# Decay levels by in-place products, GLA heads in row pairs, conditioning steps between projections

## The chip, the cores and the metric

The program runs on one core of one Trainium2 chip. The metric is the device time of one execution in microseconds (us), lower is better. TensorE is called PE here, VectorE DVE, ScalarE ACT, GpSimd POOL; SP is the queue that issues the weight transfers.

## The reference, cut to what matters

One decoder layer (`DEPTH = 1`) for 256 prompt tokens and 8 sample tokens (one new token of each of 8 sequences, which have a stored state), width 1024, all in float32:

```python
mod = (silu(c) @ w_ada + b_ada)[:, None, :]           # w_ada 1024 x 6144: "conditioning"
sh1, sc1, g1, sh2, sc2, g2 = split(mod, 6)
h = rms_norm(x, norm1_g) * (1.0 + sc1) + sh1
hq, hf, hi, hg, gq, gk, gv, gg, gr = split(h @ w_in)  # 4 HGRN2 heads 128x128, 4 GLA heads 64x128
log_f = logaddexp(log(lb), log1p(-lb) + log_sigmoid(hf))      # k_h = (1-lb) * sigmoid(-hf)
log_a = log_sigmoid(gr @ w_gk2 + b_gk2) / 16.0                # gr has 16 columns
# per head and token: S_t = diag(a_t) S_{t-1} + k_t v_t^T ; o_t = S_t^T q_t, with a = exp(log_f) or exp(log_a)
x = x + g1 * (concat(o_h, o_g) @ w_o)                 # o after a head norm and a silu gate
h = rms_norm(x, norm2_g) * (1.0 + sc2) + sh2
x = x + g2 * moe_ffn(h)                               # 32 experts, top 4, clamped SwiGLU, D_FF = 1024
y = rms_norm(x, final_norm_g)
```

The new states of the prompt and of the 8 samples are outputs too.

## The kernel before

**Two parts.** A front (conditioning, projections, recurrence, output projection, router) is followed by 32 experts in a row, each of which is applied to a gathered block of 64 tokens. The weights go through one ring in SBUF of 16 slots of 1 MB. The front loads its 42 blocks of 1 MB through slots 0 to 7 in the order of the table `FRONT`: 24 blocks of w_ada (three rounds of 8), 14 of w_in (two for each group of 512 columns), 4 of w_o. SP issues them strictly in this order, and each waits until the block that was in its slot eight loads earlier has been used (L390). Slots 8 to 15 are scratch for the recurrence (`scr`: cumulated logs, level factors, attention, values, sample states). The experts take pairs of slots (L400): 6 loads of 2 MB for each expert. The first two go into slots 0 to 3 as these come free; the third waits for `heads_out` (the outputs of all heads have left scratch, L1564) and for the stored sample states, and the others follow.

**The order of the front.** The table `MIDDLE` gives the order of tasks on PE, ACT and DVE alike; each engine walks through it and does its share. Task names: `proj c i` is one of 28 projections of 128 columns, 8 matmuls (L904); `ada r` is a round of conditioning, 8 steps of 4 matmuls into four column groups (L861), and its transposition back (L870); `low` and `y` are the gate of rank 16 (L912, L916); `lev g l` is level l of the recurrence of group g (0: HGRN2, 1: GLA; L953, L945); `vt` turns the values to tokens (L928), `kdt` the decayed keys (L961); `state` makes the prompt's states (L968, L976); `so u` reads out the sample states of unit u (L1004, L1008), u = 0 to 3 an HGRN2 head, 4 and 5 a pair of GLA heads; `out` computes the heads' outputs (L991, L994). All 4 x 8 outputs of the groups go through three PSUM banks (`aux_bank`).

**The recurrence before.** With b the cumulated log decay in a chunk of 128 tokens, level 0 is the diagonal of the attention; level l = 1 to 7 covers pairs of tokens in neighbouring halves of a block of 2m, m = 1, 2, 4, ..., 64. For each level DVE subtracts b at the block's middle (L1382, L1384), ACT takes the exponential (L660), DVE multiplies q and k by it into copies (L1400, L1404, for GLA four masked copies, L1410), PE multiplies, and DVE takes the result over under a mask (L1424). GLA heads have 64 rows of keys: two lie in one tile of 128 rows, and a mask of halves makes a full copy for each.

**The sample states** are POOL's. For each unit u in turn it issues the load of the states and of the values, spread over all partitions from a buffer in DRAM (L511 to L517), waits for both, does three operations of 128x1024 (L523, L525, L526) and stores. There are two buffers, so unit u waits for the read-out of unit u-2:

```python
if u >= 2:
    pool.wait_ge(sem("osam_done"), u - 1)
```

Read literally, unit 2 starts after `so 0` on PE and unit 3 after `so 1`. In front of unit 0 and of unit 4 POOL writes the values of the group to DRAM and waits for that (L501).

## Time and profile before

| | |
|---|---|
| three runs | 2350.32, 2345.37, 1259.42 us; median 2345.37 us |
| the profiled execution | 1259.53 us, its span 1257.8 us |
| mean granted TensorE clock in it | 0.965 |
| PE busy | 1149.9 us (91%) |
| DVE busy | 440.0 us (35%) |
| ACT, POOL busy | 202.2 us, 66.0 us |
| moved by DMA | 460.80 MB, mean 366 GB/s |

All rows below are of the profiled execution. In the chain of waits each line is a stretch of the path that ended last: when it began, how long it took, which engine and line of the kernel it was spent on ("DMA" is a wait for a transfer). A timeline lists the instructions themselves.

### The profile page before, as it was taken

The numbers are of one execution on the slowest core, as the hardware profiler recorded it, in microseconds if no ns is written. First come the engines' busy times: TensorE is split into PE (matmuls) and PEld (weight loads), VectorE is DVE, ScalarE is ACT, GpSimd is POOL, SyncE is SP. The second block draws the span as 40 slices with busy tenths as digits, with TensorE's granted clock in tenths as the row PEclk, the third lists the DMA queues.
The fourth block names the chain that finished last, engine by engine and source line by source line (L and its number), as shares of the span: only waits on it lengthen the run. The fifth ranks groups of instructions, "written<-read, shape, count | busy, mean of one in ns | idle before, by whom it ended". The sixth has DMA issues, their size and how long they took to land.

```text
span 1257.8 us, 14110 instructions
## 1 busy us (share of the span) xinstructions
PE 1149.9 (91%) x5573; PEld 535.5 (43%) x5573; DVE 440.0 (35%) x805; ACT 202.2 (16%) x361; POOL 66.0 (5%) x75
## 2 busy tenths in 40 slices
PE   6997998988999999999999998999999999999995
PEld 4753887867433333333333333333333333333331
DVE  2123876533332233432222324232233322222224
ACT  2120321121211111211111111111111111111112
POOL 0003235200000000000000000000000000000001
PEclk9997997897999999999999998999999999999998
DMA  9869764463499999999999999999999999999994
GB/s 349 305 249 363 225 151 128 137 267 134 185 427 430 426 427 429 426 430 428 427 430 427 428 430 425 429 427 425 429 427 426 429 429 427 430 427 428 430 427 180
DMA packets 46628, 460.80 MB, mean 366 GB/s; under 512 B 6677, under 2 KB 7529, under 8 KB 18906
## 3 DMA queue, kind: packets, MB, share of 16 engines
q1 hardware_dynamic: 40600, 449.69, 85.5%
q0 software_dynamic: 2752, 9.47, 3.5%
q10 hardware_dynamic: 3234, 1.05, 0.4%
q8 instruction: 29, 0.48, 0.1%
q14 instruction: 13, 0.11, 0.0%
HBM read 455.55 MB, written 4.65 MB: 366 GB/s over the span
## 4 chain that ended last, share of the span: by engine, by line
PE 59%; DMA 33%; DVE 5%; ACT 2%; ACTq 1%; issue 1%; DVEq 0%; SPq 0%
DMA ring<-in_w_up 30%; PE bank L1133 21%; PE bank L1180 12%; PE bank L904 7%; PE bank L1169 3%; PE bank L1102 3%; DMA ring<-in_w_ada 2%; PE bank L1031 2%; PE bank L1149 2%; PE bank L945 1%; PE bank L1121 1%; PE bank L861 1%; PE bank L834 1%; DVE ring L1410 1%; DVE ring L1400 1%
## 5 line engine op out<-in xcount | busy, mean ns | idle before, releaser
L1133 PE MATMUL bank<-ring,arena 128*64 128x512 f32 x2048 | 459.1, 598 | 48.2 <-DMA ring<-in_w_up 46.9
L1133 PEld LDWEIGHTS bank<-ring,arena 128*64 128x64 f32 x2048 | 142.1, 137 | 358.1 <-issue 274.5
L1180 PE MATMUL bank<-ring,arena 128*64 128x512 f32 x1024 | 228.9, 600 | 1.7 <-DVE arena L1704 1.7
L1180 PEld LDWEIGHTS bank<-ring,arena 128*64 128x64 f32 x1024 | 71.2, 138 | 136.8 <-issue 123.8
L904 PE MATMUL bank<-arena,ring 128*128 128x264 f32 x448 | 109.5, 404 | 1.8 <-DVE arena L1343 1.8
L1684 DVE COPY arena<-bank 128x512 f32<-128x512 f32 x32 | 22.1, 691 | 237.7 <-PE bank L1133 237.7
L750 ACT ACTIVATE arena<-bank 128x512 f32<-128x512 f32 x32 | 19.1, 597 | 492.4 <-PE bank L1133 492.4
L904 PEld LDWEIGHTS bank<-arena,ring 128*128 128x128 f32 x448 | 88.2, 200 | 17.7 <-issue 2.4
L1736 DVE TENSOR_TENSOR arena<-bank,arena 128x512 f32<-128x512 f32 x32 | 22.1, 691 | 194.2 <-PE bank L1180 194.2
L1731 DVE TENSOR_TENSOR arena<-arena,bank 128x512 f32<-128x512 f32 x128 | 79.1, 680 | 1.5 <-PE bank L1169 1.5
L1693 DVE TENSOR_TENSOR arena<-bank,bupT 128x512 f32<-128x512 f32 x64 | 44.0, 687 | 71.0 <-PE bank L1149 71.0
L1169 PE MATMUL bank<-arena 64*128 64x512 f32 x256 | 63.6, 615 | 1.7 <-DVE arena L1747 1.7
L1102 PE MATMUL bank<-arena 128*64 128x512 f32 x256 | 60.5, 593 | 1.0 <-DVE arena L1633 1.0
L1639 DVE TENSOR_TENSOR arena<-arena 128x256 f32<-128x256 f32 x32 | 13.6, 425 | 103.8 <-PE bank L1158 103.7
L538 POOL TENSOR_TENSOR arena<-arena 128x512 f32<-128x512 f32 x1 | 1.3, 1262 | 925.2 <-DVE arena L1747 925.2
L764 ACT ACTIVATE arena<-bank 128x256 f32<-128x256 f32 x32 | 12.2, 382 | 212.8 <-PE bank L1158 212.8
L1149 PEld LDWEIGHTS bank<-ident,arena 128*128 128x128 f32 x256 | 33.2, 209 | 26.8 <-issue 25.2
L1149 PE MATMUL bank<-ident,arena 128*128 128x128 f32 x256 | 39.2, 296 | 0.8 <-ACT arena L750 0.8
L945 PE MATMUL bank<-ring 128*128 128x64 f32 x224 | 29.4, 288 | 10.2 <-DVE ring L1410 9.6
L861 PE MATMUL bank<-ring 128*32 128x512 f32 x192 | 26.3, 672 | 10.1 <-DMA ring<-in_w_ada 10.1
L945 PEld LDWEIGHTS bank<-ring 128*128 128x128 f32 x224 | 28.8, 205 | 13.2 <-DVE ring L1410 11.3
L1102 PEld LDWEIGHTS bank<-arena 128*64 128x64 f32 x256 | 18.4, 137 | 37.0 <-issue 35.9
(278 smaller groups left out, 842.3 us busy)
## 6 DMA issues: line engine op xcount, KB each, us to landing
ring<-in_w_up SPq DMA_DIRECT2D x128, 2048.0 KB, 33.7
ring<-in_w_down SPq DMA_DIRECT2D x64, 2048.0 KB, 31.3
ring<-in_w_ada SPq DMA_DIRECT2D x24, 1024.0 KB, 12.8
ring<-in_w_in SPq DMA_DIRECT2D x14, 1024.0 KB, 20.9
ring<-in_w_o SPq DMA_DIRECT2D x4, 1024.0 KB, 7.0
ring<-in_state_hgrn POOLq DMA_DIRECT2D x4, 512.0 KB, 7.6
arena<-sample_values POOLq DMA_DIRECT2D x4, 512.0 KB, 12.4
out_hgs<-ring POOLq DMA_DIRECT2D x4, 512.0 KB, 5.4
```

The lines of the kernel that those rows point to most:

```text
L861: last = mm(bank[32 * g:32 * g + 32, 1, :], siluT[:, k, :], ring[:, FRONT_SLOT[n], 512 * g:512 * g + 512], start=(k == 0), stop=(k == KT - 1))
L904: last = mm(bank[:, b, 0:T], ring[:, slot, 512 * (k % 4) + P * i:512 * (k % 4) + P * i + P], hT[:, k, :], start=(k == 0), stop=(k == KT - 1))
L945: last = mm(bank[:, b, P * h + 64 * c:P * h + 64 * c + 64], ks[:, l % 2, h, P * c:P * c + P], qs[:, l % 2, q0:q0 + 64], start=True, stop=True)
L1031: last = mm(bank[:, WO_BANK[m % 3], 0:T], ring[:, FRONT_SLOT[ld], D * (k % 2) + P * m:D * (k % 2) + P * m + P], oT[:, k, :], start=(k == 0 ...
L1102: last = mm(bank[64 * half:64 * half + 64, 6, :], pick[:, i, :], h2tok[:, i, 512 * half:512 * half + 512], start=(i == 0), stop=(i == 1))
L1133: last = mm(bank[64 * half:64 * half + 64, b, :], xe[:, par, k % 4, k // 4, :], pairs[:, slot, col:col + 512], start=(k == 0), stop=(k == ...
L1149: last = tr(bank[:, 2 + b, P * j:P * j + P], us[:, c0:c0 + 4 * P - 3:4], ident[:, :])
L1169: mm(bank[:, b, :], gpickT[64 * half:64 * half + 64, P * i:P * i + P], ysb[64 * half:64 * half + 64, :], start=True, stop=True).then_inc(s ...
L1180: last = mm(bank[64 * half:64 * half + 64, 5, :], actT[:, k, :], pairs[:, slot, D * kk + 512 * half:D * kk + 512 * half + 512], start=(k = ...
L1684: v.tensor_copy(us[:, 512:1024], bank[:, 1, :]).then_inc(sem("us_dve"), 1)
L1693: return TT(dst.rearrange("p (j h s) -> p j h s", j=4, h=2), bank[:, 2 + b, :].rearrange("p (j h s) -> p j h s", j=4, h=2), bias(b).to_bro ...
L1731: TT(y, y, bank[:, b, :], ALU.add).then_inc(sem("acc_used"), 1)
```

## The change

- `FRONT` and `MIDDLE`: the w_ada blocks of round 1 are loaded behind the first two column groups of w_in, those of round 2 behind two more; the conditioning steps stand two by two between projections, and `turn r` is the transposition back. The levels start in the third group of projections.
- The decays themselves take the place of their logs: ACT makes a = exp(log) once (`fT`), DVE makes the products over blocks of 2, 4, ..., 128 tokens (`spans_of`, seven dependent products), and before each level multiplies q in the later halves and k in the earlier halves in place (`level_up`). The exponentials of each level, the sums, the separate copies, `kmask`, `kd` and `qdec` go: q and k end as what `out` and `kdt` need.
- GLA heads are multiplied as row pairs: 64 rows of the tile each, into a bank each, with no masked copies. A GLA level takes two banks.
- `low` writes four groups of 32 columns at once and leaves their sum to `y`.
- The conditioning vectors are loaded as 72x128 and turned by one transposition; four steps of round 0 run ahead of the norm's sums. Small loads move from SP to ACT's queue, those for the gate and the router to later.
- In the code behind the 32 experts, for tokens beyond an expert's capacity, one wait and one count are added.

POOL's own list of instructions stays as it was: 6 units with the same waits on `osam_done`. Only the place of `so 0` to `so 5` among PE's tasks moves.

```diff
 FRONT = ([("ada", 0, k) for k in range(8)]
-         + [("in", c, s) for c in (1, 0, 2) for s in range(2)]
-         + [("ada", 1, k) for k in range(8)] + [("ada", 2, k) for k in range(8)]
-         + [("in", c, s) for c in (4, 5, 3, 6) for s in range(2)]
+         + [("in", c, s) for c in (1, 0) for s in range(2)]
+         + [("ada", 1, k) for k in range(8)]
+         + [("in", c, s) for c in (2, 4) for s in range(2)]
+         + [("ada", 2, k) for k in range(8)]
+         + [("in", c, s) for c in (5, 3, 6) for s in range(2)]
          + [("out", 0, s) for s in range(4)])
...
-MIDDLE = ([("proj", c, i) for c in (HF, HQ, HI) for i in range(4)]
-          + [("ada", 1), ("vt", 0), ("ada", 2)]
-          + [("low",), ("lev", 0, 0), ("proj", GQK, 0), ("lev", 0, 1), ("proj", GQK, 1), ("lev", 0, 2),
-             ("proj", GQK, 2), ("lev", 0, 3), ("proj", GQK, 3), ("lev", 0, 4), ("y", 0), ("y", 1), ("proj", GV, 0),
-             ("lev", 0, 5), ("proj", GV, 1), ("lev", 0, 6), ("so", 0), ("proj", GV, 2), ("lev", 0, 7)]
-          + [("proj", GV, 3), ("so", 1), ("vt", 1)]
-          + [("proj", HG, 0), ("lev", 1, 0), ("proj", HG, 1), ("lev", 1, 1), ("kdt",), ("proj", HG, 2), ("lev", 1, 2),
-             ("so", 2), ("proj", HG, 3), ("lev", 1, 3), ("proj", GG, 0), ("lev", 1, 4), ("so", 3), ("proj", GG, 1),
-             ("lev", 1, 5), ("proj", GG, 2), ("lev", 1, 6), ("proj", GG, 3), ("lev", 1, 7),
-             ("state",), ("so", 4), ("so", 5), ("out",)])
+MIDDLE = ([("proj", HF, i) for i in range(4)]
+          + [t for i in range(4) for t in (("proj", HQ, i), ("ada", 1, 2 * i), ("ada", 1, 2 * i + 1))]
+          + [("turn", 1), ("proj", HI, 0), ("proj", HI, 1), ("lev", 0, 0), ("proj", HI, 2), ("lev", 0, 1),
+             ("proj", HI, 3), ("lev", 0, 2), ("low",), ("vt", 0), ("proj", GQK, 0), ("ada", 2, 0), ("ada", 2, 1),
+             ("lev", 0, 3), ("proj", GQK, 1), ("ada", 2, 2), ("ada", 2, 3), ("y", 0), ("y", 1),
+             ("lev", 0, 4), ("proj", GQK, 2), ("ada", 2, 4), ("ada", 2, 5), ("lev", 0, 5),
+             ("proj", GQK, 3), ("ada", 2, 6), ("ada", 2, 7), ("lev", 0, 6), ("turn", 2),
+             ("proj", GV, 0), ("lev", 0, 7), ("proj", GV, 1), ("lev", 1, 0), ("proj", GV, 2), ("lev", 1, 1),
+             ("proj", GV, 3), ("lev", 1, 2), ("vt", 1), ("proj", HG, 0), ("lev", 1, 3), ("proj", HG, 1), ("lev", 1, 4),
+             ("proj", HG, 2), ("so", 0), ("lev", 1, 5), ("proj", HG, 3), ("lev", 1, 6), ("proj", GG, 0), ("lev", 1, 7),
+             ("proj", GG, 1), ("kdt",), ("so", 1), ("proj", GG, 2), ("state",), ("so", 2), ("proj", GG, 3),
+             ("so", 3), ("so", 4), ("so", 5), ("out",)])
...
     if task[0] == "lev":
-        return 2 if task[2] == 0 else 1
+        return 2 if task[2] == 0 or task[1] == 1 else 1
...
-            act.wait_ge(sem("craw_zero"), 1)
-            act.dma_start(craw[0:1, :], a["c_prompt"]).then_inc(sem("c_in"), 16)
-            act.dma_start(craw[1:1 + TS, :], a["c_sample"]).then_inc(sem("c_in"), 16)
+            act.dma_start(craw[0:8, :], a["c_prompt"].rearrange("b (k p) -> (b k) p", p=P)).then_inc(sem("c_in"), 16)
+            act.dma_start(craw[8:72, :], a["c_sample"].rearrange("b (k p) -> (b k) p", p=P)).then_inc(sem("c_in"), 16)
...
-            act.dma_start(wgr, a["w_in"][0].rearrange("(k p) n -> p k n", p=P)[:, :, 3584:3600]).then_inc(sem("gr_in"), 16)
-            act.dma_start(wgk2, a["w_gk2"][0]).then_inc(sem("gr_in"), 16)
-            act.dma_start(wrt[:, :, :], a["router_w"][0].rearrange("(k p) n -> p k n", p=P)).then_inc(sem("router_in"), 16)
-            act.dma_start(brt[:, :], a["router_b"].to_broadcast([P, NE])).then_inc(sem("router_in"), 16)
...
-                if task == ("proj", HI, 3):
                     act.wait_ge(sem("logk_ready"), 1)
+                    od.did(A(fT[:, 0:4, :], fT[:, 0:4, :], ACT.Exp), sem("f_ready"))
                     od.did(A(kT[:, 0:4, :], kT[:, 0:4, :], ACT.Exp), sem("k_ready"))
-                    od.did(A(decay_s[:, 0:4, :], logf[:, 0:4, TP:T], ACT.Exp), sem("decay_s_ready"))
-                if task[0] == "ada":
-                if task[0] == "lev" and task[2] < 7:
-                    levels += 1
-                    act.wait_ge(sem("level_sub"), levels)
-                    v = level_factors(task[1], task[2] + 1)[2]
-                    od.did(A(v, v, ACT.Exp), sem("level_exp"))
...
-                if task == ("proj", GV, 3):
+                if task == ("turn", 2):
-                    od.did(A(decay_s[:, 4:6, :], logf[:, 4:6, TP:T], ACT.Exp), sem("decay_s_ready"))
-                    act.wait_ge(sem("kd_sub"), 1)
-                    od.did(A(kd[:, :, :], kd[:, :, :], ACT.Exp), sem("kd_exp"))
-                    od.did(A(decay_c[:, :], bT[:, :, TP - 1], ACT.Exp), sem("kd_exp"))
-                    od.did(A(qdec[:, 0:NQ, :], bT[:, :, P:TP], ACT.Exp), sem("kd_exp"))
+                    od.did(A(fT[:, 4:6, :], fT[:, 4:6, :], ACT.Exp, scale=1.0 / 16.0), sem("f_ready"))
+                if task == ("proj", GV, 2):
+                    act.dma_start(wrt[:, :, :], a["router_w"][0].rearrange("(k p) n -> p k n", p=P)).then_inc(sem("router_in"), 16)
+                    act.dma_start(brt[:, :], a["router_b"].to_broadcast([P, NE])).then_inc(sem("router_in"), 16)
...
-                        pe.wait_ge(sem("gr_in"), 32)
+                        pe.wait_ge(sem("gr_in"), 80)
-                            last = mm(bank[0:16, b, 0:T], wgr[:, k, :], hT[:, k, :], start=(k == 0), stop=(k == KT - 1))
+                            j = k % 4
+                            last = mm(bank[32 * j:32 * j + 32, b, 0:T], wgr[:, k, :], hT[:, k, :], start=(k < 4), stop=(k >= 4))
                         last.then_inc(sem("proj_psum"), 1)
...
+                    elif l == 0:
+                        pe.wait_ge(sem("proj_sb"), PROJ_AT[("proj", GQK, 3)] + 1)
+                        pe.wait_ge(sem(f"level_ready{g}"), 2 * l - 1)
+                    def later(x):
+                        return halves(x, l)[:, 0, :, 1, :] if l else x[:, 0, :]
+                    n = 64 if l else P
+                    if g == 1:
+                        banks = [aux_bank(), aux_bank()]
+                        for q in range(2):
+                            for c in range(NC):
+                                tt = slice(P * c, P * c + P)
+                                for i in range(2):
+                                    own = slice(64 * i, 64 * i + 64)
+                                    c0 = n * (2 * q + c)
+                                    last = mm(bank[:, banks[i], c0:c0 + n], kT[own, 4 + q, tt], later(qT[own, 4 + q:5 + q, tt]),
+                                              start=True, stop=True)
+                                    if (q, c) == (1, 1):
+                                        last.then_inc(sem("aux_psum"), 1)
...
+                    if u == 4:
+                        pe.wait_ge(sem("qsam_ready"), 4)
...
+            def spans_of(g):
+                n0, n1 = (0, 4) if g == 0 else (4, 6)
+                for l in range(1, 8):
+                    od.settle()
+                    x = spans[l - 1][:, n0:n1].rearrange("p n (q f) -> p n q f", f=2)
+                    od.did(TT(spans[l][:, n0:n1], x[:, :, :, 0], x[:, :, :, 1], ALU.mult))
+            def level_up(g, l):
+                n0, n1 = (0, 4) if g == 0 else (4, 6)
+                q, k = qT[:, n0:n1, 0:TP], kT[:, n0:n1, 0:TP]
+                ready = sem(f"level_ready{g}")
                 od.settle()
                 if l == 0:
+                    od.did(TT(q, q, fT[:, n0:n1, 0:TP], ALU.mult), ready)
                 else:
                     m = LEVELS[l - 1]
+                    shape = [P, n1 - n0, TP // (2 * m), m]
+                    x = spans[l - 1][:, n0:n1].rearrange("p n (q f) -> p n q f", f=2)
+                    late, early = halves(q, l)[:, :, :, 1, :], halves(k, l)[:, :, :, 0, :]
+                    od.did(TT(late, late, x[:, :, :, 0].unsqueeze(3).to_broadcast(shape), ALU.mult), ready)
+                    od.did(TT(early, early, x[:, :, :, 1].unsqueeze(3).to_broadcast(shape), ALU.mult), ready)
+            def level_take(g, l):
+                banks = [aux_in() for _ in range(aux_units(("lev", g, l)))]
+                level_up(g, l)
+                for n, b in enumerate(banks):
+                    own = slice(4 + 2 * n, 6 + 2 * n) if g else slice(0, 4)
+                    if l == 0:
+                        dst = att[:, own] if g else att[:, own, n, :]
+                        src = bank[:, b, :].rearrange("p (h t) -> p h t", h=4)
+                        if g:
+                            dst = dst.rearrange("p h c t -> p (h c) t")
+                        od.did(TT(dst, src, ident[:, :].unsqueeze(1).to_broadcast([P, 4, P]), ALU.mult), sem("aux_used"))
+                    else:
+                        m, x = LEVELS[l - 1], 4 if g else 8
+                        od.did(v.copy_predicated(
+                            att[:, own].rearrange("p h c (q f i) -> p (h c) q f i", f=2, i=m)[:, :, :, 1, :],
+                            level_mask[:, l - 1, :].rearrange("p (q f i) -> p q f i", f=2, i=m)[:, :, 1, :].unsqueeze(1)
+                            .to_broadcast([P, x, P // (2 * m), m]),
+                            bank[:, b, 0:64 * x].rearrange("p (x q i) -> p x q i", x=x, i=m)), sem("aux_used"))
```

**PE, from the read-out of the second sample unit to the outputs of the heads.** L1004 and L1008 in the kernel before are the read-outs (`so`), L904 a projection, L945 a level, L961 `kdt`, L968 and L976 `state`, L991 `out`. Before, from `so 1` on:

```order
L1004 MATMUL bank<-arena,ring 128x1 x8
L928 MATMUL bank<-ident,arena 128x128 x8
L928 MATMUL bank<-ident,arena 8x128 x4
L904 MATMUL bank<-arena,ring 128x264 x8
L953 MATMUL bank<-arena 128x128 x8
L904 MATMUL bank<-arena,ring 128x264 x8
L945 MATMUL bank<-ring 128x64 x8
L961 MATMUL bank<-ident,arena 128x128 x12
L904 MATMUL bank<-arena,ring 128x264 x8
L945 MATMUL bank<-ring 128x64 x8
L1004 MATMUL bank<-arena,ring 128x1 x8
L904 MATMUL bank<-arena,ring 128x264 x8
```

and its end, from `so 3` on:

```order
L1004 MATMUL bank<-arena,ring 128x1 x8
L904 MATMUL bank<-arena,ring 128x264 x8
L945 MATMUL bank<-ring 128x64 x8
L904 MATMUL bank<-arena,ring 128x264 x8
L945 MATMUL bank<-ring 128x64 x8
L904 MATMUL bank<-arena,ring 128x264 x8
L945 MATMUL bank<-ring 128x64 x8
L968 MATMUL bank<-ring 128x128 x8
L976 MATMUL bank<-ring 64x128 x8
L1008 MATMUL bank<-qsam,ring 128x2 x16
L991 MATMUL bank<-ring 128x128 x5
```

Of the change, from the last level on, where L918 is a projection, L968 a GLA level, L993 `kdt`, L1045 and L1049 read-outs, L1000 and L1008 `state`, L1020 `out`:

```order
L968 MATMUL bank<-arena 128x64 x8
L918 MATMUL bank<-arena,ring 128x264 x8
L993 MATMUL bank<-ident,arena 128x128 x12
L1045 MATMUL bank<-arena,ring 128x1 x8
L918 MATMUL bank<-arena,ring 128x264 x8
L1000 MATMUL bank<-ring 128x128 x8
L1008 MATMUL bank<-ring 64x128 x8
L1045 MATMUL bank<-arena,ring 128x1 x8
L918 MATMUL bank<-arena,ring 128x264 x8
L1045 MATMUL bank<-arena,ring 128x1 x8
L1049 MATMUL bank<-qsam,ring 128x2 x16
L1020 MATMUL bank<-ring 128x128 x5
```

Before, eight projections and eight levels lie behind `so 1`; now `so 1` has two projections behind it, and all levels lie ahead.

**PE, from the conditioning round 0 to the first values.** Before (L861 conditioning, L870 its transposition, L904 projections, L928 `vt`):

```order
L861 MATMUL bank<-ring 32x512 x32
L870 MATMUL bank<-ident,ring 128x128 x4
L904 MATMUL bank<-arena,ring 128x264 x96
L861 MATMUL bank<-ring 32x512 x32
L870 MATMUL bank<-ident,ring 128x128 x4
L928 MATMUL bank<-ident,arena 128x128 x8
L928 MATMUL bank<-ident,arena 8x128 x4
L861 MATMUL bank<-ring 32x512 x32
L870 MATMUL bank<-ident,ring 128x128 x4
```

Of the change (L853 conditioning, L884 its transposition, L918 projections, L977 level 0):

```order
L884 MATMUL bank<-ident,ring 128x128 x4
L918 MATMUL bank<-arena,ring 128x264 x40
L853 MATMUL bank<-ring 32x512 x8
L918 MATMUL bank<-arena,ring 128x264 x8
L853 MATMUL bank<-ring 32x512 x8
L918 MATMUL bank<-arena,ring 128x264 x8
L853 MATMUL bank<-ring 32x512 x8
L918 MATMUL bank<-arena,ring 128x264 x8
L853 MATMUL bank<-ring 32x512 x8
L884 MATMUL bank<-ident,ring 128x128 x4
L918 MATMUL bank<-arena,ring 128x264 x16
L977 MATMUL bank<-arena 128x128 x8
```

Rounds 1 and 2 stood together behind twelve projections; now round 1 lies between the projections of the second group, and its last two steps with the transposition stand right behind them.

**SP, the front's loads.** `waits` names what a load waits for. Of the change:

```order
L407 DMA ring<-in_w_in 128x4x512 [waits weights_used] x4
L407 DMA ring<-in_w_ada 128x2048 [waits weights_used] x3
L407 DMA ring<-in_w_ada 128x2048 [waits ada_psum]
L407 DMA ring<-in_w_ada 128x2048 [waits weights_used]
L407 DMA ring<-in_w_ada 128x2048 [waits proj_psum]
L407 DMA ring<-in_w_ada 128x2048 [waits weights_used]
L407 DMA ring<-in_w_ada 128x2048 [waits proj_psum]
L407 DMA ring<-in_w_in 128x4x512 [waits weights_used] x4
```

The last two w_ada loads of a round take the slots of the projection group that runs right ahead of the steps that use them, and the next w_in blocks stand behind them in SP's queue.

## Rows read from the trace of the kernel before

**Rows 1.** the page: the whole span, and GB/s in 40 equal slices
```profile
span 1257.8 us, 14110 instructions
...
GB/s 349 305 249 363 225 151 128 137 267 134 185 427 430 426 427 429 426 430 428 427 430 427 428 430 425 429 427 425 429 427 426 429 429 427 430 427 428 430 427 180
```

**Rows 2.** windows: start:end, us, busy (count) by engine, clock, DMA share, GB/s
```profile
400.00:500.00 100.00, 100.00 (x475) 36.35 (x472) 31.10 (x55) 12.63 (x23) 0.00 (x0) 1.00 1.01 428
```

**Rows 3.** DMA issues: what, queue, count, KB each, median us to landing
```profile
ring<-in_w_up SPq DMA_DIRECT2D x128, 2048.0 KB, 33.7
ring<-in_w_down SPq DMA_DIRECT2D x64, 2048.0 KB, 31.3
```

**Rows 4.** chain of waits: start us, us, what; last read-outs to first expert
```profile
241.80 4.89 PE bank L1008 x32
246.69 2.34 PE bank L991 x10
...
255.01 0.23 DVE arena L1564
...
325.70 15.65 PE bank L1133 x64
```

**Rows 5.** chain of waits, opening of the kernel up to the third projection group
```profile
14.79 1.22 DVE ring L1301
...
25.48 7.05 PE bank L861 x64
...
35.69 44.66 PE bank L904 x192
80.36 7.11 DMA ring<-in_w_ada
...
110.24 1.98 PE bank L861 x8
```

**Rows 6.** chain of waits: projection, level, sample read-out; an expert's combine
```profile
121.49 3.56 PE bank L904 x16
125.06 1.73 PE bank L945 x16
...
166.64 1.68 PE bank L1004 x16
```

**Rows 7.** timeline of DVE and ACT behind the second projection group
```profile
72.75 1.26 DVE L1461 TENSOR_TENSOR arena<-arena 128x1056 f32<-128x1056 f32 x1
...
80.72 1.07 ACT L650 ACTIVATE arena<-arena 128x1056 f32<-128x1056 f32 x1
```

**Rows 8.** timeline of POOL: start us, us, instruction, idle before it, releaser
```profile
175.35 0.88 POOL L511 DMA_DIRECT2D ring<-in_state_hgrn  x1
...
186.92 1.89 POOL L523 TENSOR_TENSOR arena<-arena 128x1024 f32<-128x1024 f32 x1 [9.81 <-DMA arena<-sample_values]
...
194.64 0.54 POOL L501 DMA_DIRECT2D sample_values<-ring  x1
...
210.62 1.90 POOL L523 TENSOR_TENSOR arena<-arena 128x1024 f32<-128x1024 f32 x1 [6.29 <-DMA arena<-sample_values]
...
218.61 0.70 POOL L511 DMA_DIRECT2D ring<-in_state_gla  x1
...
227.95 1.89 POOL L523 TENSOR_TENSOR arena<-arena 128x1024 f32<-128x1024 f32 x1 [6.60 <-DMA arena<-sample_values]
...
234.67 1.43 POOL L528 DMA_DIRECT2D out_gls<-ring  x2 [0.29 <-POOL ring L526]
```

**Rows 9.** timeline of DVE: one operation, POOL idle and POOL at work
```profile
179.82 0.42 DVE L1400 TENSOR_TENSOR ring<-arena,ring 128x256 f32<-128x256 f32 x1
...
187.03 2.06 DVE L1400 TENSOR_TENSOR ring<-arena,ring 128x256 f32<-128x256 f32 x1
```

**Rows 10.** a projection that began at the lower clock, and that stretch
```profile
200.92 6.46 PE bank L904 x16
...
190.00:204.00 14.00, 10.07 (x39) 9.35 (x40) 8.56 (x15) 1.84 (x5) 7.23 (x8) 0.60 0.21 59
```

356 lines of the change are left out of this document (150 added, 206 removed).

## The prediction

> **What bounds the kernel now.** I read the windows first. While the experts run, DMA is busy throughout and moves 428 GB/s [rows 1, 2]. Their weights are (128 + 64) transfers of 2048 KB, 402.7 MB [rows 3], and 402.7 MB at 428 GB/s are 941 us. PE runs beside it with less work than that: it is full only as long as the loads fetched ahead last. The 192 loads are six for each of 32 experts, so the code for overflowing tokens isn't entered. The change leaves this part alone, so its end follows one point: when the first expert starts and ring pairs come free. That is at 325.7 us; the heads are finished (L1564) at 255.2 us [rows 4], and the same instructions fill the 70.5 us between. So a microsecond by which the heads are finished earlier or later should be a microsecond of the whole. Everything in dispute lies before 255.2 us.
>
> The chain through the front shows why it takes that long. PE starts the projections at 35.7 us, does the first twelve in 44.7 us, and then waits for w_ada: rounds 1 and 2 end at 112.2 us instead of 80.4 us plus 14 us of work [rows 5]. From there PE is nearly full, with waits for DVE while POOL works.
>
> **The change part by part.** Times below are counted from the start of the span.
>
> *Opening.* ACT made three operations of 32x1024 behind its queue of DMA issues, DVE one, and PE's wait for it ended at 16.0 us [rows 5]. These become 72x128, about an eighth of the elements, and half of round 0 (7.05 us in all) runs ahead of the norm's sums. But w_ada's own 8.4 MB behind 1 MB of x, at the 349 GB/s of the first slice [rows 1], land only near 27 us, and about 1 us of conditioning and 3.2 us of copy, transposition and scaling follow as before. I take the first projection at 32.5 us (gain 3.2); bounds 31.2 and 35.7.
>
> *Groups HF and HQ.* Eight projections at 44.66 / 12 = 3.72 us are 29.8, six conditioning steps at 7.05 / 8 = 0.88 are 5.3: T1 = 67.6.
>
> *First refill.* Steps 6 and 7 of round 1 need slots that the projections of HQ right ahead of them free. The trace has this very pattern: two w_ada blocks behind twelve projections, the last one in after 7.1 us [rows 5]. The next blocks in SP's order are 1.05 MB each, 2.45 us at 428 GB/s; both HI blocks are in at T1 + 12.0. ACT agrees: it now makes both exponentials (1.07 us each) ahead of the copy for the transposition. DVE's last operation on the logs ended 8.6 us behind HQ (35.7 + 8 x 3.72 = 65.4 against 74.0) [rows 7]; plus 2.2 for the exponentials and 1.3 for copy and transposition that is T1 + 12.1. PE does the rest of HI 0 by T1 + 16.0 = 83.6.
>
> *Work to the end of GQK.* Seven projections 26.0, six conditioning steps 5.3, six levels at 1.73 10.4 [rows 6]. `vt` has twelve small matmuls and is put at a level's 1.7; `low` in four column groups and `y` are ten more, concurrent or short, at 1.0 each. Sum 45.4, T2 = 129.0. DVE's share for an HGRN2 level is two multiplications and the take-over, 512 elements each, about 0.7 between the rows of 256 and of 1056 elements [rows 7, 9], against 5.5 us of PE between two levels, and hides; if it didn't, PE would wait for it. The ACT exponentials of levels, DVE's sums, scans and masked copies that go are off PE's path, except where POOL is at work. New ahead of level 0 are seven dependent products of some 1,000 elements in all, about 2 us by the row of 1056, beside HI's projections.
>
> *Second refill.* Steps 6 and 7 of round 2 behind GQK: the same pattern, 7.1 us, with the last GV block in at T2 + 12.0; GV 0 ends, with the level ahead of it, at T2 + 14.5 = 143.5.
>
> *Work to `so 1`.* Nine projections 33.5, one HGRN2 level 1.7, eight GLA levels, `vt` and `kdt` 1.7 each, two read-outs at 1.68 3.4 [rows 6]. A GLA level keeps its eight matmuls, now with 64 rows. The nearest row for such pairs is the experts' combine, eight with 64 rows and 512 columns in 1.92 us [rows 6]; bounds for a level are half of 1.73 and 2.0; I take 1.4, so 11.2. Sum 53.2: 196.7. To this I add 5 us of waits and lower clock, bounds 0 and 14 (three times the clash and twice the clock that follow). A DVE operation took 0.42 us with POOL idle and 2.06 us with POOL at work [rows 9], and three POOL units now fall into the levels. A projection that began at the lower level took 6.46 us against 3.56; the granted clock in 190 to 204 us was 0.60, behind two waits of PE [rows 6, 10]; its two levels are 2.4 and 1.2 GHz, and each refill is such a wait. `so 1` ends at about 202.
>
> *The sample states.* Here the change gives the gain back. Unit 3 needs `so 1`, 4 follows 3, 5 follows 4, all on POOL, whose own work isn't changed. The rows give the price: from the issue of unit 3 (175.35) to the end of unit 5 (0.3 before 234.67) 59.0 us. In it are 9.81, 6.29 and 6.60 us of waits for transfers, three times 6.4 of arithmetic, and the detour of group 1's values through DRAM, 194.64 to over 200 [rows 8]. Before, `so 1` ended at 168.3 us [rows 6] and eight projections and eight levels covered the 59 us; POOL ended at 234.4, and PE came to the last two units at 241.8 [rows 4]. Now PE has two projections, `state` and four read-outs to put over them, some 20 us. So PE waits: 202 + 0.5 + 59 = 261.5. Unit 2 doesn't add: `so 0` ends 19 us ahead of `so 1`, and unit 2 takes the 18 of unit 3 (175.35 to 193.4) and its store. Then come `so 5` (half of 4.89), `out` and the last copies (246.7 to 255.2 before, 8.5 us [rows 4]; I take 11 behind such a long wait): 275. Against 255.2 this is +19.8. For a clock that stays low a little into the norm I add 1.5. The profiled execution's own time is 1259.53, 1.7 above its span: 1259.5 + 21.3 = **1281 us**.
>
> One rule would make the chain shorter. The waits of POOL for its transfers were 9.81, 6.29 and 6.60 us, for 1 MB and twice 0.5 MB [rows 8]. The Trainium skill ("DMA: Bandwidth & Descriptors", section on the anatomy of one DMA) gives about 2.0 us plus bytes / 436e3 for one DMA; by it these waits would be 4.4, 3.2 and 3.2 us, the chain 47 us and the time about 1269. The trace disagrees with it for these spread-out values of 512 bytes, and I go by the rows.
>
> The rest is small: router and gate weights move to later on ACT's queue and are covered by the projections that stand ahead of their users; if that were gone, each would cost about the 7.1 us of a load that PE waits for. `so 4`'s new wait on the masked queries is over long before.
>
> **The rivals.**
> - *The state chain doesn't decide* (0.12). Then PE's own work does: 202 + 3.7 + 3.5 (`state`, sixteen matmuls, as two levels) + 1.7 + 3.7 + 1.7 + 4.9 + 8.5 = 229.7, 25.5 us earlier than before: 1234. For it: DVE lies idle there, nothing slows POOL. Against: 59 us are three times what PE has left; the chain would have to fall to under 30.
> - *The balance is nearly even* (0.12), 1250 to 1265: GLA levels at half price (4 us), no waits (5 us), transfers of the states at 6 us (3 us), refills shorter by some.
> - *`so 1` comes late* (0.18), 1294 to 1310: since all of POOL's chain hangs on it, each wait of PE ahead of it is paid in full, and so it decides the sign beyond 2% from about 206 us on. The clash of DVE and POOL, 6.4 us of slowed DVE in each of three units, would hold PE up by up to some 4 us each time, while GLA levels stand in line for their banks, and the clock would follow.
> - *That the change isn't what it says*: order shows the read-outs where I put them; I give this nothing.
>
> The forecast itself, 1266 to 1294, has 0.58.
>
> **How the numbers follow.** What a measurement of this kernel can tell from no change is about 2%, 25 us, so the limits are 1234 and 1285. Faster: a half of the first rival, 0.06. Slower: nearly all of the third, 0.17, and the upper 0.4 of the forecast, 0.24, in all 0.41. The rest, 0.53, lies within. The likeliest case's own range is 1266 to 1294, that of all cases 1245 to 1300. The sum stands against 1259.53 us, the profiled execution, with which one of the three runs (1259.42) agrees; the median shown, 2345.37, is that of the other two, 1.86 times longer. Such a ratio is near that of the two clock levels, and I can't tell from one profile which of them a median of the changed kernel will hit; I give the longer 0.35. There the front's PE work doubles and POOL's chain doesn't, so my gain and loss would lie between 2345 - 45 and 2345 + 45, about twice the limits above. A range that leaves out no more than 2 in 10 has to reach that far: 1245 to 2390.
>
> **What would show it.** In the changed trace: the first projection near 32.5 us; waits for w_ada of some 5 to 7 us behind HQ and behind GQK; read-out L1045 waiting for POOL at the fourth, fifth and sixth unit, with PE nearly idle from about 217 to 261 us; heads finished near 275 and the first expert's L1174 near 346. I am wrong if PE doesn't wait for POOL there, if `so 1` ends before 190 or after 210, or if the experts don't shift one for one with the heads.

## The result and the profile after

The changed kernel takes 1283.63 us (median of 4 runs, 1282.61 to 1285.38). Its ratio to the kernel before is **1.0177, 95% interval 1.0118 to 1.0237**: slower; whether by more or less than 2% is not settled. Beside it the kernel before ran in two groups again (1252.69 and 1259.42, 2345.37 and 2350.32); the ratio leaves the long group out, no run of the changed kernel fell into it, and against the two short runs alone it would be 1.022. The profiled execution took 1283.37 us.

The page of the kernel after, the rows that answer to [rows 1]:

```profile
span 1281.5 us, 14019 instructions
...
PEclk9989899569799999999999999899999999999999
...
GB/s 347 292 321 107 313 174 153 149 124 186 106 378 429 428 426 428 427 429 429 428 429 429 429 428 429 428 426 428 428 427 429 426 430 429 428 429 428 429 429 181
```

The full rate of 428 GB/s begins one slice later than before; behind it the rates are the same within 2 GB/s. A slice is 32 us, and the change lies in that one and the slices ahead of it. PE's waits (in total, times, longest):

```profile
PE bank L1174 <- DMA ring<-in_w_up: 47.9, 41, 1.3
PE bank L1049 <- POOL ring L543: 31.3, 2, 17.4
PE bank L853 <- DMA ring<-in_w_ada: 18.4, 5, 10.2
...
PE bank L1045 <- POOL ring L543: 4.6, 1, 4.6
```

35.9 us of waits for POOL in the sample read-outs. They lie here (timeline of PE, the last projections to the output products):

```profile
206.23 1.50 PE L993 MATMUL bank<-ident,arena 128*128 128x128 f32 x12 [2.94 <-issue]
207.56 1.84 PE L1045 MATMUL bank<-arena,ring 128*128 128x1 f32 x16
209.27 3.81 PE L918 MATMUL bank<-arena,ring 128*128 128x264 f32 x16
...
226.00 3.58 PE L1045 MATMUL bank<-arena,ring 128*128 128x1 f32 x16 [4.57 <-POOL ring L543]
246.94 3.55 PE L1049 MATMUL bank<-qsam,ring 128*128 128x2 f32 x16 [17.36 <-POOL ring L543]
264.43 3.57 PE L1049 MATMUL bank<-qsam,ring 128*128 128x2 f32 x16 [13.94 <-POOL ring L543]
```

The first row is `kdt`, the second `so 1`, the last three are `so 3`, `so 4` and `so 5`. POOL's timeline shows what they wait for, and answers to [rows 8]:

```profile
187.58 0.88 POOL L528 DMA_DIRECT2D ring<-in_state_hgrn  x1 [38.96 <-PE bank L1045]
...
209.72 0.88 POOL L528 DMA_DIRECT2D ring<-in_state_hgrn  x1 [2.64 <-PE bank L1045]
...
219.72 1.89 POOL L540 TENSOR_TENSOR arena<-arena 128x1024 f32<-128x1024 f32 x1 [8.24 <-DMA arena<-sample_values]
...
231.84 0.73 POOL L528 DMA_DIRECT2D ring<-in_state_gla  x1 [4.12 <-DMA sample_values<-ring]
...
240.63 1.89 POOL L540 TENSOR_TENSOR arena<-arena 128x1024 f32<-128x1024 f32 x1 [5.94 <-DMA arena<-sample_values]
...
258.21 1.89 POOL L540 TENSOR_TENSOR arena<-arena 128x1024 f32<-128x1024 f32 x1 [6.99 <-DMA arena<-sample_values]
...
264.67 1.43 POOL L545 DMA_DIRECT2D out_gls<-ring  x2 [0.29 <-POOL ring L543]
```

POOL stood idle for 38.96 us until `so 0` freed a buffer. Then units 3, 4 and 5 followed each other from 209.72 to 264.4 us, 54.7 us, and PE had 12 us of projections, `state` and `so 2` (209.27 to 221.4) to put over them. In the windows (columns as in [rows 2]) PE does 0.58 us of work in 17, and its clock falls to the lower level:

```profile
229.00:246.00 17.00, 0.58 (x3) 0.49 (x3) 0.00 (x0) 0.00 (x0) 8.06 (x7) 0.50 0.37 89
```

The chain of waits, which answers to [rows 4], runs from POOL through `so 5` into the experts:

```profile
262.04 2.35 POOL ring L543
264.43 3.57 PE bank L1049 x16
268.00 2.34 PE bank L1020 x10
...
350.88 13.95 PE bank L1174 x64
```

### The profile page after: what moved, and what is told of

It is laid out like the page before. It is cut to its first block, busy times and chain, and to the rows that moved or that the text cites. A ratio compares the mean times of both kernels' runs of the same rounds, so it can differ in the third digit from the quotient of the medians.

```text
span 1281.5 us, 14019 instructions
## 1 busy us (share of the span) xinstructions
PE 1134.8 (89%) x5566; PEld 518.7 (40%) x5566; DVE 393.8 (31%) x756; ACT 189.0 (15%) x344; POOL 65.6 (5%) x75
## 4 chain that ended last, share of the span: by engine, by line
PE 46%; DMA 30%; DVE 1%; ACT 1%; POOL 0%; issue 0%; SPq 0%; DVEq 0%; ACTq 0%
DMA ring<-in_w_up 30%; PE bank L1174 20%; PE bank L1221 12%; PE bank L1143 3%; PE bank L1210 3%; PE bank L1072 2%; PE bank L1190 2%; PE bank L1162 1%; PE bank L1199 1%; DMA arena<-sample_values 1%; PE bank L1090 0%; PE bank L1116 0%; PE bank L1020 0%; PE bank L1049 0%; PE bank L1056 0%
## 5 line engine op out<-in xcount | busy, mean ns | idle before, releaser
L918 PE MATMUL bank<-arena,ring 128*128 128x264 f32 x448 | 108.5, 399 | 1.8 <-DVE arena L1382 1.8
L918 PEld LDWEIGHTS bank<-arena,ring 128*128 128x128 f32 x448 | 85.7, 196 | 19.4 <-issue 4.6
L555 POOL TENSOR_TENSOR arena<-arena 128x512 f32<-128x512 f32 x1 | 1.3, 1267 | 925.3 <-DVE arena L1732 925.3
L853 PE MATMUL bank<-ring 128*32 128x512 f32 x192 | 28.3, 712 | 18.8 <-DMA ring<-in_w_ada 18.4
L1049 PE MATMUL bank<-qsam,ring 128*128 128x2 f32 x32 | 7.1, 352 | 31.3 <-POOL ring L543 31.3
L1210 PEld LDWEIGHTS bank<-arena 64*128 64x128 f32 x256 | 26.8, 185 | 16.6 <-issue 10.5
```

Source lines behind the costliest of these rows:

```text
L853: last = mm(bank[32 * g:32 * g + 32, 1, :], siluT[:, k, :], ring[:, FRONT_SLOT[n], 512 * g:512 * g + 512], start=(k == 0), stop=(k == KT - 1))
L918: last = mm(bank[:, b, 0:T], ring[:, slot, 512 * (k % 4) + P * i:512 * (k % 4) + P * i + P], hT[:, k, :], start=(k == 0), stop=(k == KT - 1))
L1210: mm(bank[:, b, :], gpickT[64 * half:64 * half + 64, P * i:P * i + P], ysb[64 * half:64 * half + 64, :], start=True, stop=True).then_inc(s ...
```

## The experiments

The yardstick is DVE's copy of the sample columns ("heads"), the last thing before the norm; before it began at 255.0 us, after at 278.3 us (278.28, L1549). "Heads" and the spans are those of one profiled execution of each kernel; the medians are over all its runs. The kernel before, timed beside each group of experiments, had medians of 1260.09, 1261.38 and 1260.53 us.

### so_early: only the read-outs move back

```diff
-             ("proj", GV, 0), ("lev", 0, 7), ("proj", GV, 1), ("lev", 1, 0), ("proj", GV, 2), ("lev", 1, 1),
+             ("proj", GV, 0), ("lev", 0, 7), ("so", 0), ("proj", GV, 1), ("lev", 1, 0), ("so", 1), ("proj", GV, 2), ("lev", 1, 1),
...
-             ("proj", GG, 1), ("kdt",), ("so", 1), ("proj", GG, 2), ("state",), ("so", 2), ("proj", GG, 3),
-             ("so", 3), ("so", 4), ("so", 5), ("out",)])
+             ("so", 3), ("proj", GG, 1), ("kdt",), ("proj", GG, 2), ("state",), ("proj", GG, 3),
+             ("so", 4), ("so", 5), ("out",)])
```

`so 2` stands behind `lev 1 4`, and the places between projections where the change had `so 0` to `so 2` are empty.

> The changed kernel with its read-outs moved: so 0 and so 1 right behind GV 0 and GV 1, so 2 behind the fifth GLA level, so 3 behind the last level. Theory (POOL's chain of sample states, 55 us from so 1 to the end of unit 5, sets the end): it starts near 155 instead of 209.7 us, unit 5 is ready near 231 us, heads at about 245, time about 1250 us. Rival (the levels, the refills or the clock set the end, and the read-outs wait only beside it): less than 10 us gained, 1274 us or more.

1256.85 us (10 runs), ratio 0.9967 (0.9931 to 1.0002). Heads at 251.7 us, 26.6 us earlier than in the change, and the span is shorter by 27.0 us. That is the theory's way, though 245 and 1250 had been expected. One wait for POOL is left:

```profile
PE bank L1049 <- POOL ring L543: 6.8, 1, 6.8
```

So the whole loss is the read-outs' place. But the rest of the change, which I had counted as a gain, brought only 3.3 us over the kernel before, and the ratio's interval reaches 1.

### before_so_late: the kernel before with late read-outs

```diff
-             ("lev", 0, 5), ("proj", GV, 1), ("lev", 0, 6), ("so", 0), ("proj", GV, 2), ("lev", 0, 7)]
-          + [("proj", GV, 3), ("so", 1), ("vt", 1)]
...
+             ("lev", 0, 5), ("proj", GV, 1), ("lev", 0, 6), ("proj", GV, 2), ("lev", 0, 7)]
+          + [("proj", GV, 3), ("vt", 1)]
+          + [("proj", HG, 0), ("lev", 1, 0), ("proj", HG, 1), ("lev", 1, 1), ("kdt",), ("proj", HG, 2), ("so", 0), ("lev", 1, 2),
...
+             ("so", 1), ("lev", 1, 5), ("proj", GG, 2), ("lev", 1, 6), ("so", 2), ("proj", GG, 3), ("lev", 1, 7),
+             ("state",), ("so", 3), ("so", 4), ("so", 5), ("out",)])
```

> The kernel before with nothing changed but the place of so 0 to so 3: as late among the projections as the change has them (so 0 behind HG 2, so 1 behind GG 1, so 2 behind GG 2, so 3 behind the last level). Theory: so 1 ends near 218 us, POOL's chain of 55 to 59 us ends near 275, heads near 289 instead of 255, time about 1292 us (1283 to 1300). Rival (the cost comes with the new arithmetic or the interleaved conditioning): no change, 1259 us.

1287.22 us (4 runs), ratio 1.0177 (1.0099 to 1.0255). Nothing of the new arithmetic is in it, and the same wait stands in the same place:

```profile
PE bank L1008 <- POOL ring L526: 31.8, 2, 17.8
```

Heads at 289.9 us, 34.9 us late, span 34.7 us longer. The profiled execution (1294.36 us) was the slowest of the four; the medians differ by 27 us.

### five_buffers: the late read-outs stay, the buffers don't run out

```diff
-        Ssam = scr[:, 13312:15360].rearrange("p (u b v) -> p u b v", u=2, b=TS)
+        NSB = 5
+        Ssam = [scr[:, c:c + 1024].rearrange("p (b v) -> p b v", b=TS) for c in (13312, 14336, 15360, 3584, 4864)]
...
-                if u >= 2:
-                    pool.wait_ge(sem("osam_done"), u - 1)
+                if u >= NSB:
+                    pool.wait_ge(sem("osam_done"), u - NSB + 1)
```

> The changed kernel in its own order, with five buffers for the sample states instead of two, so that only unit 5 waits for a read-out (so 0). Theory: POOL runs its units through and is done near 224 us, PE meets all read-outs ready; its waits of 36 us behind so 1 go, heads near 241, time about 1245 us (1240 to 1250). Rival (POOL's transfers and arithmetic are the bound themselves, not the wait for the read-outs): 1270 us or more.

1258.74 us (10 runs, one of them 1484.87), ratio 0.9963 (0.9927 to 1.0000). The mechanism is confirmed: with buffers to spare the same late order costs nothing against before. The expected 1245 is missed, though. The profiled execution, at 1267.47 us, is 9 us above the median, so its rows may show more waiting than most runs had. PE's wait for POOL became shorter but not gone:

```profile
PE bank L1050 <- POOL ring L544: 20.1, 1, 20.1
```

POOL itself is the next bound. It cannot start before unit 0's values are turned (109.7 us), and from the third on a unit takes 22 to 25 us beside the weight loads, with waits for transfers of 12.6 to 16.4 us.

### new_arith_old_order: the arithmetic alone

```diff
-MIDDLE = ([("proj", HF, i) for i in range(4)]
-          + [t for i in range(4) for t in (("proj", HQ, i), ("ada", 1, 2 * i), ("ada", 1, 2 * i + 1))]
+MIDDLE = ([("proj", c, i) for c in (HF, HQ, HI) for i in range(4)]
+          + [("ada", 1, k) for k in range(8)] + [("turn", 1), ("vt", 0)] + [("ada", 2, k) for k in range(8)] + [("turn", 2)]
...
```

Levels, read-outs and the order of the loads are those of the kernel before; only `kdt` stands behind the last level and `y` behind GQK 1.

> The in-place products, row pairs and column groups of the change, in the order of the kernel before: rounds 1 and 2 of the conditioning together behind twelve projections, read-outs where they were; kdt behind the last level, the gate's y behind GQK 1. Theory: the arithmetic by itself gains the DVE waits (about 10 us), 0.7 us for each of 8 GLA levels and some 4 us of the low-rank gate, while the pause of 32 us stays: 1243 us (1238 to 1250), with no long wait for POOL. Rival (the new arithmetic costs DVE or PE time): 1262 us or more.

1252.80 us (10 runs), ratio 0.9946 (0.9909 to 0.9983). Heads at 244.7 us, 10.3 us earlier than before, and no wait for POOL. The times gain less (7 us between the medians, 6.9 between the spans), and 1243 had been expected. POOL starts at 89.85 us:

```profile
89.85 0.72 POOL L514 DMA_DIRECT2D sample_values<-ring  x1 [85.95 <-DVE ring L1488]
```

The products of block decays and the row pairs are a gain, then. In so_early the heads are 7 us later than here. The two kernels differ in the order of conditioning and projections, but also in the places of levels and read-outs, so these 7 us are not shown to be the first alone; between the spans they are 3.6, because the first expert's 64 matmuls (L1170) took 16.85 us here, at 0.82 granted, and 13.95 in so_early, at 1.00.

### short_units: shorter work in the chain

```diff
+                if u < 3:
+                    od.did(g.tensor_tensor(vbc[:, :, :], vbc[:, :, :],
+                                           kT[:, u, TP:T].unsqueeze(2).to_broadcast([P, TS, P]), ALU.mult))
+                    od.link(g.tensor_tensor(S, S, fT[:, u, TP:T].unsqueeze(2).to_broadcast([P, TS, P]), ALU.mult))
```

> The change, with GpSimd's two multiplications left out in units 3 to 5 (the sample states of those units keep only their load and the addition, so part of the decode states isn't computed). Nothing else moves. In the change's trace the chain from the issue of unit 3's load (209.72) to the end of unit 5's work (264.4) is what the fourth, fifth and sixth read-outs wait for (4.6, 17.4 and 13.9 us). Theory 1 (the state chain, one unit after another behind the late second read-out, ends the stage): three units lose some 3.8 us each, the chain 11.3 us, the heads and the end come 11 us earlier: about 1272 us. Theory 2 (the projections and conditioning matmuls set the stage, and the waits for GpSimd would only be replaced by others): no more than 3 us, 1280 to 1283.

1278.44 us (2 runs), ratio 1.0126 (1.0075 to 1.0177); heads at 271.8 us, 6.5 us earlier than in the change, not 11. Its POOL rows say why:

```profile
212.45 0.88 POOL L528 DMA_DIRECT2D ring<-in_state_hgrn  x1 [2.64 <-PE bank L1046]
...
234.26 0.74 POOL L528 DMA_DIRECT2D ring<-in_state_gla  x1 [7.75 <-DMA sample_values<-ring]
...
258.99 1.40 POOL L546 DMA_DIRECT2D out_gls<-ring  x2 [0.29 <-POOL ring L544]
```

Unit 3 was issued 2.7 us later than in the change, and the values' detour through DRAM waited 7.75 us instead of 4.12. From issue to end the chain takes 46.3 us instead of 54.7, 8.4 shorter; less the 2.7 that is 5.7, and the heads moved by 6.5. Theory 2 (at most 3 us) is out, and theory 1's 11 us are missed. The chain sets the end; what a cut of it gives back also depends on the transfers. Why the detour took longer was not tested.

### no_interleave: conditioning steps in one piece

```diff
-MIDDLE = ([("proj", HF, i) for i in range(4)]
-          + [t for i in range(4) for t in (("proj", HQ, i), ("ada", 1, 2 * i), ("ada", 1, 2 * i + 1))]
+MIDDLE = ([("proj", c, i) for c in (HF, HQ) for i in range(4)]
+          + [("ada", 1, k) for k in range(8)]
...
-             ("lev", 0, 4), ("proj", GQK, 2), ("ada", 2, 4), ("ada", 2, 5), ("lev", 0, 5),
-             ("proj", GQK, 3), ("ada", 2, 6), ("ada", 2, 7), ("lev", 0, 6), ("turn", 2),
...
+             ("lev", 0, 4), ("proj", GQK, 2), ("lev", 0, 5), ("proj", GQK, 3)]
+          + [("ada", 2, k) for k in range(8)]
+          + [("lev", 0, 6), ("turn", 2),
```

> The change with the conditioning steps 0 to 7 of groups 1 and 2 put together again behind the four projections of their stage (HQ and GQK) instead of two between each pair; the read-outs of the sample states, the levels and their arithmetic stay as in the change. Theory 1 (each refill of the conditioning weights waits for the slots that the steps free, and is covered less or more by what runs beside it, and GpSimd's start hangs on the value turn of unit 0): the stage loses waits for GpSimd's start of some 10 us, the second read-out and the chain behind it come about 10 us earlier, 1273 us. Theory 2 (the place of the conditioning steps is worth nothing, only the place of the read-outs is): 1281 to 1285, as the change.

1272.74 us (6 runs), ratio 1.0092 (1.0059 to 1.0125). Heads at 266.8 us, 11.5 us earlier, as theory 1 said. POOL started 7.0 us earlier, and unit 3's load was issued at 197.58 instead of 209.72 us, right behind unit 2 and without a wait for `so 1`. With the steps between the projections PE has used them up when the refill's last blocks are still on their way; in one piece, most of the steps run while it loads. In the changed kernel the last blocks of group 1 and of group 2 (timeline of PE):

```profile
73.71 1.07 PE L853 MATMUL bank<-ring 128*32 128x512 f32 x8 [3.38 <-DMA ring<-in_w_ada]
77.86 1.94 PE L853 MATMUL bank<-ring 128*32 128x512 f32 x8 [3.09 <-DMA ring<-in_w_ada]
...
143.67 1.94 PE L853 MATMUL bank<-ring 128*32 128x512 f32 x8 [10.22 <-DMA ring<-in_w_ada]
```

and in no_interleave, where seven of the eight steps of group 2 (56 matmuls) run in one piece ahead of the last; 4.49 us of waiting come behind it, for the values' weights:

```profile
120.20 6.22 PE L854 MATMUL bank<-ring 128*32 128x512 f32 x56
128.39 1.27 PE L854 MATMUL bank<-ring 128*32 128x512 f32 x8 [1.98 <-DMA ring<-in_w_ada]
...
138.61 5.86 PE L919 MATMUL bank<-arena,ring 128*128 128x264 f32 x16 [4.49 <-DMA ring<-in_w_in]
```

### combined and combined_late_loads

`combined` is no_interleave with five buffers, the read-outs of so_early, and `so 4`, `so 5` behind `out`. The second also holds back SP:

```diff
                 elif expert_slot(i) < 4:
+                    if i == 0:
+                        sp.wait_ge(sem("Ssam_ready"), NQ)
                     for half in range(2):
```

> The conditioning steps put together as in no_interleave, the read-outs 0 to 3 each as soon as its unit is ready and the last two behind the output products, and five buffers for the sample states instead of two. Theory 1 (the two causes, the late start of GpSimd and the read-outs' hold on the buffers, add up, and the last two units lie behind work that does not need them): the heads start at about 237, the time is 1241 us. Theory 2 (GpSimd's own chain of load, work and store beside the experts' first weights stays the bound, as in five_buffers): 1250 to 1258.

1247.51 us (4 runs), ratio 0.9881 (0.9843 to 0.9919); heads at 241.7 us, 5 later than expected, with 11.1 us of waiting for POOL. The time lies between the two theories.

> As combined, but SyncE issues the experts' first two weight loads only when the sample states of the last unit are ready. Theory 1 (the transfers of the states are slow because they share the DMA engines with these weights): units fall from some 25 us to some 17, and the time is 1235 to 1240 us, a few us below combined. Theory 2 (the first experts would then wait for their weights): the first expert's products start later by as much as the weights come late, 1245 to 1255 us, at or above combined.

1246.29 us (4 runs), ratio 0.9864 (0.9824 to 0.9904), which can't be told from combined. The transfer of unit 4 did what theory 1 says. First combined, then combined_late_loads (POOL's timeline):

```profile
210.01 1.89 POOL L542 TENSOR_TENSOR arena<-arena 128x1024 f32<-128x1024 f32 x1 [15.24 <-DMA arena<-sample_values]
```

```profile
201.96 1.89 POOL L544 TENSOR_TENSOR arena<-arena 128x1024 f32<-128x1024 f32 x1 [6.42 <-DMA arena<-sample_values]
```

POOL was done 12.5 us earlier, but PE came to the last two read-outs at 233.59 instead of 225.03 us. It was 2.4 us behind when the projection after `so 3` began, which took 5.40 us where combined had 3.81; a wait for DVE ahead of the last output products was 3.47 instead of 2.01 us, and these products ran at a granted 0.56 (226 to 234 us, PE busy 7.45 of 8). Theory 2's wait for the experts' weights did not appear: PE's waits for w_up are 46.9 us in all, against 47.3 in combined. What POOL's chain gave back, PE's own pace took; why the pace fell was not tested.

### early_values, and with late loads

Against combined, cut:

```diff
-         + [("in", c, s) for c in (1, 0) for s in range(2)]
+         + [("in", c, s) for c in (1, 0, 2) for s in range(2)]
...
-MIDDLE = ([("proj", c, i) for c in (HF, HQ) for i in range(4)]
-          + [("ada", 1, k) for k in range(8)]
+MIDDLE = ([("proj", c, i) for c in (HF, HQ, HI) for i in range(4)]
+          + [("ada", 1, k) for k in range(8)]
+          + [("turn", 1), ("vt", 0), ("lev", 0, 0), ("low",), ("proj", GQK, 0), ("lev", 0, 1), ("proj", GQK, 1), ("y", 0), ("y", 1),
...
```

The weights of HI are loaded ahead of round 1 with it, and every level stands one or two projections later than in combined.

> As combined (new arithmetic, five buffers, read-outs early, the last two behind the output products), and the four HI projections come before the conditioning steps of group 1 again, as in the kernel before, so that the value turn of unit 0 needs only the steps ahead of it. Theory 1 (combined is still bound by GpSimd's chain, whose start, 103, hangs on that turn): GpSimd starts at about 90, its last unit is ready before the output products end (225), the heads follow the last two read-outs at about 231, the time is 1236 us. Theory 2 (what is left is TensorE's own work at its clock, as combined_late_loads suggests, where GpSimd was 13 us earlier and the time the same): 1245 to 1248 us.

1239.14 us (4 runs), ratio 0.9844 (0.9793 to 0.9894); heads at 234.7 us, with 7.0 us of waiting for POOL left. POOL started at 91.9 us as expected, but its last unit was ready at 231.0, not before 225.

> As early_values, with SyncE's first two weight loads for the experts held until the last unit's sample states are ready. Theory 1 (with GpSimd's chain off the path by 10 us the transfers' sharing of the DMA engines no longer matters): as early_values within 3 us. Theory 2 (the chain is still the bound): 5 us below it.

**1235.09 us** (4 runs), ratio 0.9809 (0.9755 to 0.9863), heads at 228.0 us, no wait for POOL left. This is the fastest version. The intervals of the two ratios overlap, but the runs themselves don't (1231.96 to 1238.10 against 1238.16 to 1240.63 us), so the 4 us between the medians are likely real, and near theory 2's 5; the heads moved by 6.7 us. Its read-outs behind the output products took 3.80 us for both units, where one unit alone took 3.57 us at the lower clock in the change:

```profile
223.73 0.49 PE L1035 MATMUL bank<-arena 64*128 64x128 f32 x2
224.15 3.80 PE L1051 MATMUL bank<-qsam,ring 128*128 128x2 f32 x32
229.38 2.92 PE L1058 MATMUL bank<-arena,ones 128*128 128x512 f32 x3 [1.43 <-ACT arena L701]
```

All profiled executions together, in us. "POOL ends" is the end of the last unit's arithmetic:

| kernel | POOL starts | POOL ends | heads | span | span less heads |
|---|---|---|---|---|---|
| before | 92.6 | 234.4 | 255.0 | 1257.8 | 1002.8 |
| the change | 108.1 | 264.4 | 278.3 | 1281.5 | 1003.2 |
| so_early | 109.1 | 237.7 | 251.7 | 1254.5 | 1002.8 |
| before_so_late | 95.5 | 277.7 | 289.9 | 1292.5 | 1002.6 |
| five_buffers | 109.7 | 249.0 | 262.7 | 1265.4 | 1002.7 |
| new_arith_old_order | 89.9 | 230.3 | 244.7 | 1250.9 | 1006.2 |
| short_units | 107.7 | 258.7 | 271.8 | 1275.8 | 1004.0 |
| no_interleave | 101.1 | 252.6 | 266.8 | 1272.1 | 1005.3 |
| combined | 103.0 | 238.0 | 241.7 | 1245.2 | 1003.5 |
| combined_late_loads | 103.3 | 225.5 | 240.6 | 1246.8 | 1006.2 |
| early_values | 91.9 | 231.0 | 234.7 | 1237.7 | 1003.0 |
| early_values_late_loads | 90.1 | 219.5 | 228.0 | 1233.9 | 1005.9 |

The last column lies at 1002.6 to 1004.0 or at 1005.3 to 1006.2 us. In the four kernels with the higher values the first expert's 64 matmuls took 16.57 to 16.85 us, in the others 13.95 or 15.65.

## Why the prediction was right or wrong

**The mechanism held; that the time fits within 3 us is in part luck.** Forecast 1281, measured 1283.63. PE was 10 us later than forecast when GV 0 ended, and shorter levels (2.5) and a shorter chain on POOL (4.4) took most of that back. Point by point, against the trace after:

- *Bound and one-for-one shift*: right. The last column of the table stays within 1002.6 and 1006.2 us while the heads move over 62 us.
- *Opening*: wrong by all of it. I took the first projection at 32.5 us; it began at 35.46, as before. The shorter ACT work did get out of the way (PE's wait for it is gone), but conditioning went on waiting for its own weights: the last block's step began at 31.18 us behind 1.17 us of waiting for w_ada. Behind it came 1.07 us of conditioning and 3.2 us of copy, transposition and scaling, as I had them. The landing is what failed: I divided w_ada's and x's 9.4 MB by 349 GB/s, but by 31.2 us 10.8 MB had moved (345 GB/s in that window). SP had issued w_in from 17.01 us on, so its blocks were among them; no run held them back.
- *First refill*: the waits were 3.38 and 3.09 us (7.1 predicted). HI 0 started at 81.77 and ended at 87.4 (ACT's copy of it began at 87.47), against 83.6. The opening explains 3 us of that; the rest is the clock, 0.50 granted in 81.7 to 85.5 us, which the sum had left out here.
- *Second refill*: 7.1 us taken, 10.2 measured, and GV 0 ended at 153.6 instead of 143.5. GQK had ended 4.4 us late (133.4 against 129.0), so this stage lost 5.7. The trace of before showed this pattern with POOL idle. Here POOL issued the state load of unit 1 and its broadcast at 128.09 and 128.96 us, just ahead of the refill; the DMA engines were busy at 0.96 in 130 to 143 us and moved only 220 GB/s, against 362 in the first refill (windows; the columns are those of [rows 2]). That was the term with the largest error, and no row of mine counted POOL's transfers against PE's. That they are the cause is argued from these windows; no run moved that load alone.

```profile
70.00:81.00 11.00, 3.47 (x19) 0.49 (x18) 3.78 (x3) 7.43 (x9) 0.00 (x0) 0.75 0.97 362
...
130.00:143.00 13.00, 3.45 (x16) 2.61 (x14) 2.49 (x4) 0.39 (x1) 1.80 (x1) 0.76 0.96 220
```

- *Levels*: from its start to the next task a GLA level took 1.03 to 1.12 us, not 1.4 (eight levels, some 2.5 us or a little more in my favour). The waits and the clock that I put at 5 us were little more: 0.99 us within `vt`, 2.94 ahead of `kdt` (where DVE had three operations of 1.38 to 2.56 us beside POOL at work), and 1.55 for one projection of 5.38 us. `so 1` ended at 209.3 against 202, 55.7 us behind GV 0, which I had put at 58.2.
- *Sample states*: 59 us predicted, 54.7 measured, with waits of 8.24, 5.94 and 6.99 us and of 4.12 for the detour. The read-outs that wait are the fourth, fifth and sixth, as said, and PE was idle from 229.6 to 246.9 us and from 250.5 to 264.4.
- *From `so 5` to the heads*: 13.9 us, predicted 13.5. Heads 278.3 against 275.

So `so 1` was 7.4 us late, the chain 4.4 us short, and the two left 3 us. Counted at the heads, experiment so_early shows that the place of the read-outs costs 26.6 us, new_arith_old_order that the arithmetic gains 10.3, and no_interleave that the conditioning steps between projections cost 11.5 where the read-outs are late. For this last cost the forecast had no term beyond the two refills.

**The step that failed is the one from the time to the chances.** I wrote that what a measurement can tell from no change is about 2%, 25 us, without a row for it, and so gave "within 2%" the largest share, 0.53, though my own forecast, 1281 against 1259.53, is 1.7% above. The runs show a finer limit. The changed kernel's four runs lie within 0.2% of each other, and the interval of the ratio is 0.6% to each side of 1.77%, which leaves out 1; in the experiments it is 0.3 to 0.8% to each side. With a limit of 0.6% (1252 to 1267) nearly the whole forecast of 1266 to 1294 and the third rival lie on the slower side. Only for one run against one is 2% a fair figure: 25 runs of the kernel before lie between 1249.80 and 1272.63 us. Within the sum, the term that was mis-sized most is the second refill. The upper end of the range, 2390, stands for the longer times of the kernel before, to which I gave 0.35: neither the changed kernel's median nor that of any experiment lies near it.

The rule on DMA that I weighed would have made the chain 47 us. The rows after decide as those before: POOL waited 5.9 to 8.2 us. An estimate by the formula of the Trainium skill ("DMA: Bandwidth & Descriptors", section "Anatomy of one DMA") is 3.2 to 4.4 us for such sizes, and the trace disagrees with it. Even in combined_late_loads and early_values_late_loads, with the experts' weights held back, units 4 and 5 waited 5.91 to 6.55 us.

## What to carry to other kernels

A read-out that frees a buffer is a start signal for the engine behind it: moving it later "to where nothing waits for it" moves the whole producer. Before such a move, add up the producer's chain from that point (load, work, handover) and compare it with the work left to put over it. And count every load of another queue that can fall into a refill by the time for which it keeps the DMA engines busy, not by its bytes.
